# Expansion units of the next head pair between the first score steps of this one

## The chip, the cores and the metric

The kernel runs on one core of a Trainium2 chip. The time is device microseconds (us) of one execution of the program. Three executions of the kernel before took 3314.32, 3317.00 and 3317.49 us; the median is 3317.0 us. The profile is of a further execution, which took 3313.17 us; its span, from the first to the last instruction, is 3311.3 us. The engines are TensorE (PE; PEld is its weight load), VectorE (DVE), ScalarE (ACT), GpSimd (POOL) and the queue SyncE (SP).

## The reference, cut to what matters

Two layers over 1024 latent and 128 context tokens of width 1024: a short gated convolution and a multi-head latent attention, each followed by a squared-ReLU MLP. The change touches only the attention of the second layer. It has 16 heads of 96 query and key values (64 plus 32 rotary) and 64 values:

```python
q = (rmsnorm(h @ w_dq, q_norm_g) @ w_uq).reshape(b, n, N_HEADS, QK_DIM);  q = rmsnorm(q, qn_g)
kn, v = jnp.split((ckv @ w_ukv).reshape(b, n, N_HEADS, QK_NOPE + V_DIM), [QK_NOPE], axis=-1)
k = rmsnorm(jnp.concatenate([kn, kpe], -1), kn_g)          # then the rotary part of q and k
s = jnp.einsum('bqhd,bkhd->bhqk', qblk, k) * scale
p = jax.nn.softmax(s, axis=-1);  o = jnp.einsum('bhqk,bkhd->bqhd', p, v)
```

The latent tokens attend to themselves and to 128 cached keys, the context tokens to themselves.

## The kernel before, in words

Every product of 32-bit values is made of three matmuls (`three`, L814 to L822): each operand is kept as a high part and a low part, and high*high, high*low and low*high are summed. ACT makes the high parts, DVE or GpSimd the low ones.

The heads are worked in 8 pairs. Seven pairs run in a hardware loop, the eighth is written out with `last=True`. Each engine has its own program of a pair, and semaphores tie them. The parts of a pair are:

- **Value units.** 3 units of TensorE (60 matmuls of 128x128) make v of both heads for all 10 key tiles; ACT and DVE take it out as v_hi and v_lo.
- **Turn units of head 1.** 6 units of transposes turn q_tok (9 tiles) and k_tok (10 tiles) into qT and kT; ACT makes qT_hi and kT_hi, DVE qT_lo and kT_lo.
- **Expansion units** (`qk_units`, 8 units). They make q and k of the *next* pair: 5 query units (81 matmuls of 192 columns) and 3 key units (60 of 128 columns). ACT copies each to q_tok or k_tok and squares it in place in PSUM, DVE sums the squares (ssq). On DVE the program puts between the sums the normalisation of the previous pair (`over_sums`, 5 pieces: a reciprocal of the row sums, and a multiplication of o), and the rotary part of the queries (`rotate`, twice).
- **Score steps.** Positions 0 to 37, 19 of each head: 18 of 512 columns and one of 128. Position pos makes scores of position pos+3 (3 matmuls into bank 3 or 4), and the values product of position pos (3 matmuls). Between them stand ACT's exponential p and its high part p_hi (`step`), and GpSimd's low part p_lo.
- **Maxima.** 9 tiles of each head: 3 matmuls write 1152 columns into banks 0 to 2 (`max_tile`), DVE reduces them to row_max (`max_out`). There is one buffer, so a tile waits for the reduction of the one before. Then row_max is transposed (`max_unit`) and DVE writes it as extra rows of qT_hi (`max_rows`); the scores of that head read these rows. Head 1's maxima are for this pair, head 0's for the next.
- **Token scaling** (`token_scale`). DVE divides q_tok and k_tok by their norms (r_tok), in parts between the reductions of head 1. ACT's square root for r_tok (`token_rstd`) needs another table than the exponential.
- **Turn units of head 0** of the next pair, at TURN_A.

All units share banks 0 to 2 in turn (`unit`): unit k waits until unit k-3 has been taken out. The maxima use the same banks, so the first tile of a head waits until every unit is taken out. The order of the work is written out by hand, per engine, by positions: before, the 8 expansion units all come ahead of position 0, a maxima tile comes every one and a half positions from position 0 and from 22 on, row maxima follow at 13 and 35, the turn of head 0 at 20. The first scores of the next pair are made at positions 36 and 37. ACT writes out sums and products of head 0 (`output`) after its steps 17, 21 and 22.

## Time and profile before

| what | value |
|---|---|
| median of three runs | 3317.0 us |
| profiled execution, and its span | 3313.17 us, 3311.3 us |
| TensorE busy | 3070.7 us, 93% of the span |
| VectorE, ScalarE, GpSimd busy | 1469.5, 1011.1, 855.9 us |
| slices of the span with TensorE at 7 to 8 tenths | those of the attention (about 1500 to 2370 us) |

A busy time is an average over stages with different limits. In the slices of the two MLPs TensorE shows 9 tenths or more; in those of the attention 7 or 8. "Idle before" in a row is the time in which the engine did nothing before the instruction, and the name behind the arrow is what ended that wait. Matmuls overlap, so the duration of a single one is longer than its share; the start of one to the start of the next is the share.

### The profile page before, as it was taken

How to read it: one execution, taken by the hardware profiler on the slowest of the kernel's cores; microseconds unless marked ns; L12 is line 12 of the kernel's file. 1: busy time of each engine (PE TensorE's matmuls, PEld its weight loads, DVE VectorE, ACT ScalarE, POOL GpSimd, SP SyncE). 2: the span in 40 equal slices, each digit the busy share in tenths (PEclk: the TensorE clock that was granted, in tenths of full speed). 3: DMA queues.
4: the chain of work that ended last, by engine and by line, in shares of the span. 5: the costliest groups of instructions: out<-in, count | busy, mean ns of one | idle time of the engine just before them, and what ended most of it. 6: DMA issues, size and time to landing. Idle time of an engine off the chain costs nothing.

```text
span 3311.3 us, 43718 instructions
## 1 busy us (share of the span) xinstructions
PE 3070.7 (93%) x17193; PEld 2931.1 (89%) x17193; DVE 1469.5 (44%) x1856; ACT 1011.1 (31%) x1447; POOL 855.9 (26%) x509
## 2 busy tenths in 40 slices
PE   7999998999999999877888888888898999999999
PEld 7999998999999999876777777776798999999999
DVE  2654545555544556554455554564324222222222
ACT  2211113111111112223666667556613111111111
POOL 0122111212212121111553446445421112212121
PEclk6999998999999999886999999899999999999999
DMA  4122220222111221200000000000110111111111
GB/s 192 66 84 94 75 90 32 77 77 82 63 69 64 89 76 63 93 11 7 6 7 2 7 5 7 8 6 0 77 44 26 45 39 44 44 38 39 44 44 76
DMA packets 45532, 166.60 MB, mean 50 GB/s; under 512 B 5792, under 2 KB 7456, under 8 KB 45216
## 3 DMA queue, kind: packets, MB, share of 16 engines
q1 hardware_dynamic: 44912, 160.89, 13.9%
q10 hardware_dynamic: 560, 4.87, 0.4%
q8 instruction: 43, 0.70, 0.1%
q14 instruction: 17, 0.14, 0.0%
HBM read 156.15 MB, written 9.58 MB: 50 GB/s over the span
## 4 chain that ended last, share of the span: by engine, by line
PE 61%; issue 23%; DVE 9%; ACT 4%; POOL 2%; DVEq 0%; ACTq 0%; POOLq 0%
PE ps L822 58%; PE ps L1068 2%; POOL w_lo L459 2%; DVE sums L1586 2%; DVE row_max L1568 1%; ACT p L745 1%; DVE hid_lo L1306 1%; DVE tmp L1301 1%; PE ps L1054 1%; ACT hid_hi L594 1%; ACT tmp L591 1%; DVE q_tok L1543 1%; DVE ssq L1508 0%; DVE k_tok L1548 0%; DVE x L1272 0%
## 5 line engine op out<-in xcount | busy, mean ns | idle before, releaser
L459 POOL TENSOR_TENSOR w_lo<-w_raw,w_hi 128x1024 fp32r<-128x1024 f32 (+2 forms) x190 | 463.4, 2439 | 1979.0 <-ACT w_hi L532 1979.0
L822 PE MATMUL ps<-h_hi,w_hi 128*128 128x384 f32 x2640 | 607.7, 338 | 49.5 <-DVE h_lo L1253 24.6
L822 PE MATMUL ps<-h_lo,w_hi 128*128 128x384 f32 x2640 | 604.2, 336 | 0.0
L822 PE MATMUL ps<-h_hi,w_lo 128*128 128x384 f32 x2640 | 603.1, 336 | 0.0
L822 PEld LDWEIGHTS ps<-h_hi,w_hi 128*128 128x128 f32 x2640 | 474.6, 190 | 54.0 <-issue 43.7
L475 POOL TENSOR_TENSOR p_lo<-p,p_hi 128x512 fp32r<-128x512 f32 (+1 forms) x304 | 384.2, 1273 | 433.8 <-ACT p_hi L747 429.8
L532 ACT ACTIVATE w_hi<-w_raw 128x1024 fp32r<-128x1024 f32 (+2 forms) x190 | 194.6, 1025 | 984.1 <-PE ps L822 912.1
L822 PEld LDWEIGHTS ps<-h_lo,w_hi 128*128 128x128 f32 x2640 | 475.4, 190 | 0.0
L822 PEld LDWEIGHTS ps<-h_hi,w_lo 128*128 128x128 f32 x2640 | 474.2, 189 | 0.0
L1272 DVE SCALAR_TENSOR_TENSOR x<-ps,mod,x 128x256 f32<-128x256 f32 (+5 forms) x432 | 240.1, 611 | 480.0 <-PE ps L822 478.3
L822 PE MATMUL ps<-hid_hi,w_hi 128*128 128x384 f32 x1536 | 350.4, 335 | 9.7 <-DVE hid_lo L1306 9.6
L822 PE MATMUL ps<-hid_lo,w_hi 128*128 128x384 f32 x1536 | 348.6, 334 | 0.0
L822 PE MATMUL ps<-hid_hi,w_lo 128*128 128x384 f32 x1536 | 348.5, 334 | 0.0
L1301 DVE SCALAR_TENSOR_TENSOR tmp<-ps,tmp 128x1152 f32<-128x1152 f32 x64 | 86.9, 1358 | 494.3 <-ACT tmp L591 494.3
L822 PEld LDWEIGHTS ps<-hid_hi,w_hi 128*128 128x128 f32 x1536 | 272.6, 188 | 15.1 <-DVE hid_lo L1306 14.7
L822 PEld LDWEIGHTS ps<-hid_lo,w_hi 128*128 128x128 f32 x1536 | 273.7, 188 | 0.0
L822 PEld LDWEIGHTS ps<-hid_hi,w_lo 128*128 128x128 f32 x1536 | 273.7, 188 | 0.0
L1568 DVE TENSOR_REDUCE row_max<-ps 128x1 f32<-128x1152 f32 x144 | 178.1, 1237 | 159.0 <-PE ps L1068 159.0
L591 ACT ACTIVATE tmp<-ps 128x1152 f32<-128x1152 f32 x64 | 72.6, 1135 | 531.6 <-PE ps L822 531.6
L745 ACT ACTIVATE p<-ps 128x512 f32<-128x512 f32 (+1 forms) x304 | 175.8, 578 | 160.1 <-PE ps L822 152.2
L1189 DVE CUSTOM_DVE_ANT_0 ps<-mod_raw,cond_row 128x1024 f32<-128x1024 f32 x80 | 211.7, 2646 | 1.6 <-issue 0.7
L747 ACT ACTIVATE p_hi<-p 128x512 fp32r<-128x512 f32 (+1 forms) x304 | 187.0, 615 | 9.7
(135 smaller groups left out, 3587.3 us busy)
## 6 DMA issues: line engine op xcount, KB each, us to landing
w_raw<-in_wall_dram SPq DMA_DIRECT2D x174, 512.0 KB, 3.7
mod_raw<-in_mod_rows_dram SPq DMA_DIRECT2D x80, 512.0 KB, 3.5
mod_first<-in_mod_cols_dram SPq DMA_DIRECT2D x16, 512.0 KB, 15.2
x<-in_x_t_dram SPq DMA_DIRECT2D x8, 576.0 KB, 7.6
x_spill<-x ACTq DMA_DIRECT2D x1, 4608.0 KB, 15.2
x<-x_spill SPq DMA_DIRECT2D x1, 4608.0 KB, 13.7
out_dram<-x SPq DMA_DIRECT2D x8, 576.0 KB, 2.8
w_raw<-in_wall_dram SPq DMA_DIRECT2D x8, 416.0 KB, 3.1
```

Source lines behind the costliest of these rows:

```text
L459: pool.tensor_tensor(w_lo[s][:, 0:words], w_raw[s][:, 0:words], w_hi[s][:, 0:words].bitcast(F32), ALU.subtract).then_inc(w_lo_done, 1)
L475: pool.tensor_tensor(p_lo[s][:, 0:n], p32[s][:, 0:n], p_hi[s][:, 0:n].bitcast(F32), ALU.subtract).then_inc(p_lo_done, 1)
L532: act.activation(w_hi[s][:, 0:words], w_raw[s][:, 0:words], ACT.Copy).then_inc(w_hi_done, 1)
L591: act.activation(cols3(tmp[0][:, 0:N]), stage_ps(L.at["s"]), ACT.Relu).then_inc(relu_done, 1)
L745: act.activation(p32[s][:, 0:n], bank(3 + pos % 2, n), ACT.Exp, scale=SCALE).then_inc(p_exp, 1)
L747: act.activation(p_hi[s][:, 0:n], p32[s][:, 0:n], ACT.Copy).then_inc(p_hi_done, 1)
L822: ins = pe.matmul(out, lhs[a], rhs[b](cols), start=first and n == 0, stop=last and n == 2)
L1068: ins = pe.matmul(ps[:, b0:b0 + n], qT_hi[s][0:QK, t * P:(t + 1) * P], kT_hi[s][0:QK, c0:c0 + n], start=True, stop=True)
L1189: ins = dve.tensor_tensor_reduce(product, raw, cond_row[:, c, :], 1.0, 0.0, ALU.mult, ALU.add, mod_acc[:, slot, c:c + 1])
L1272: ins = dve.scalar_tensor_tensor(xt, v, mod[:, ds(gate, 1), c:c + 1].rearrange("p a c -> p (a c)"), xt, ALU.mult, ALU.add)
L1301: dve.scalar_tensor_tensor(cols3(tmp[1][:, 0:N]), stage_ps(L.at["s"]), 0.0, cols3(tmp[0][:, 0:N]), ALU.max, ALU.mult).then_inc(stage_free, 1)
L1568: dve.tensor_reduce(row_max[:, t:t + 1], ps[:, 0:n], AX_X, ALU.max).then_inc(max_free, 1)
```

## The change: what it does

The table EXPAND says after which position which expansion unit stands: units 0 and 1 after position 0, units 2 to 7 after positions 1 to 6. A maxima tile comes every position instead of every one and a half; head 1's start at position 7 instead of 0, head 0's at 23 instead of 22. Row maxima follow at 15 and 32 instead of 13 and 35. The turn of head 0 is at 21 instead of 20. The first two scores of the next pair come after position 37. On ACT the square root comes after step 11 instead of 4, and the outputs of head 0 after steps 14, 26 and 27. On DVE the scaling parts become 7 instead of 5 (each key part is split in two) and stand behind tiles 2 to 8. The names `expand`, `q_unit`, `k_unit`, `kv_unit`, `turn_queries` and `turn_keys` cut the old loops into single units; what a unit does is the same.

```diff
-TURN_A = STEPS + 1
-MAX_B, MAX_A = 0, TURN_A + 2
-ROWS_B, ROWS_A = MAX_B + 13, MAX_A + 13
+EXPAND = [(0, 0), (0, 1), (1, 2), (2, 3), (3, 4), (4, 5), (5, 6), (6, 7)]
+TURN_A = STEPS + 2
+MAX_B, MAX_A = 7, TURN_A + 2
+ROWS_B, ROWS_A = MAX_B + 8, MAX_A + 9
...
@@ ACT, pair()
                             turn_units(U_V, 1)
-                            if not last:
-                                qk_units(U_V + U_TURN)
-                        if pos == LAG + 1 and not last:
+                        for at_pos, i in EXPAND:
+                            if pos == at_pos + LAG and not last:
+                                expand(U_V + U_TURN, i)
+                        if pos == LAG + 8 and not last:
                             token_rstd()
...
-                        if pos in (17, STEPS + 9 + LAG):
+                        if pos in (14, STEPS + 9 + LAG):
                             output(head, 0, p)
-                        if pos in (17 + LAG + 1, 18 + LAG + 1):
-                            output(0, pos - 17 - LAG, p)
+                        if pos in (TURN_A + 5, TURN_A + 6):
+                            output(0, pos - TURN_A - 4, p)
...
@@ PE, pair()
                     turn_units(U_V, 1)
                     if not last:
-                        qk_units(U_V + U_TURN)
                         A.at["tok"] += 1
-                    pe.wait_ge(unit_free, A.count("u", (0 if last else U_QK) + U_TURN))
+                    pe.wait_ge(unit_free, A.count("u", U_TURN))
                     def maxima(half):
 
                         for s, start in ((1, MAX_B), (0, MAX_A)):
-                            t, off = divmod(half - 2 * start, 3)
+                            t, off = divmod(half - 2 * start, 2)
...
                         if pos + LAG < 2 * STEPS:
                             scores(pos + LAG)
-                        elif pos > 2 * STEPS - LAG and not last:
-                            scores(pos - (2 * STEPS - LAG + 1), LAG - 1)
                         maxima(2 * pos)
                         values(pos)
                         maxima(2 * pos + 1)
+                        for at_pos, i in EXPAND:
+                            if pos == at_pos and not last:
+                                expand(U_V + U_TURN, i)
...
+                    if not last:
+                        for pos in range(LAG - 1):
+                            scores(pos, pos)
...
@@ DVE, token_scale() and pair()
-                    elif part == 3:
-                        scale_keys(0)
+                    elif part in (3, 5):
+                        scale_keys((part - 3) // 2)
                     else:
-                        scale_keys(1).then_inc(tok_ready, 1)
+                        ins = rotary_keys((part - 4) // 2)
+                        if part == 6:
+                            ins.then_inc(tok_ready, 1)
...
-                        if not last and 2 <= t < 7:
+                        if not last and t >= 2:
                             token_scale(t - 2)
```

VectorE, the end of head 1's maxima in the loop. Each TENSOR_REDUCE of row_max is one tile; the TENSOR_TENSOR rows are the scaling of q_tok and k_tok; the last row but one before is the writing of the row maxima. Before, from tile 5 on:

```order
L1568 TENSOR_REDUCE row_max<-ps 128x1
L1548 TENSOR_TENSOR k_tok<-k_tok,r_tok 128x10x64
L1549 TENSOR_TENSOR k_tok<-kpe_rot,r_tok 128x10x32
L1567 REGISTER_ALU
L1568 TENSOR_REDUCE row_max<-ps 128x1
L1548 TENSOR_TENSOR k_tok<-k_tok,r_tok 128x10x64
L1549 TENSOR_TENSOR k_tok<-kpe_rot,r_tok 128x10x32
L1567 REGISTER_ALU
L1568 TENSOR_REDUCE row_max<-ps 128x1
L1567 REGISTER_ALU
L1568 TENSOR_REDUCE row_max<-ps 128x1
L1573 REGISTER_ALU
```

After, from tile 6 on, to the writing of the row maxima:

```order
L1638 TENSOR_REDUCE row_max<-ps 128x1
L1617 TENSOR_TENSOR k_tok<-kpe_rot,r_tok 128x10x32
L1637 REGISTER_ALU
L1638 TENSOR_REDUCE row_max<-ps 128x1
L1613 TENSOR_TENSOR k_tok<-k_tok,r_tok 128x10x64
L1637 REGISTER_ALU
L1638 TENSOR_REDUCE row_max<-ps 128x1
L1617 TENSOR_TENSOR k_tok<-kpe_rot,r_tok 128x10x32
L1643 REGISTER_ALU
L1645 SCALAR_TENSOR_TENSOR qT_hi_106<-ps,ident 9x1152
```

The key parts have moved behind the last tiles: a scaling operation now stands between the last reduction and the writing of the row maxima.

TensorE, the end of head 1's maxima. `ident,row_max` is the transposition of the row maxima, `qT_hi_106` and `kT_hi_110` belong to head 1, whose first scores (position 19) they make. Before, what stands around the transposition:

```order
L822 MATMUL ps<-qT_hi_105,kT_hi_109 128x512
L822 MATMUL ps<-qT_lo_107,kT_hi_109 128x512
L822 MATMUL ps<-qT_hi_105,kT_lo_111 128x512
L822 MATMUL ps<-p_hi_118,v_hi 128x512
L822 MATMUL ps<-p_lo_117,v_hi 128x512
L822 MATMUL ps<-p_hi_118,v_lo 128x512
L1075 REGISTER_ALU
L1007 REGISTER_ALU
L1077 MATMUL ps<-ident,row_max 9x128
```

After:

```order
L1114 MATMUL ps<-kT_hi_110,qT_hi_106 128x128
L841 MATMUL ps<-p_hi_115,v_hi 128x512
L841 MATMUL ps<-p_lo_114,v_hi 128x512
L841 MATMUL ps<-p_hi_115,v_lo 128x512
L1121 REGISTER_ALU
L1026 REGISTER_ALU
L1123 MATMUL ps<-ident,row_max 9x128
L1131 REGISTER_ALU
L1133 REGISTER_ALU
L841 MATMUL ps<-qT_hi_106,kT_hi_110 128x512
L841 MATMUL ps<-qT_lo_108,kT_hi_110 128x512
```

Before, positions 14 and 15 stood between the transposition and head 1's first scores; now those scores follow it at once.

ScalarE, ahead of the turn of head 0 (`qT_hi`); `o` and `sums` are an output. Before:

```order
L760 ACTIVATE o_87<-ps 64x512
L761 ACTIVATE sums<-ps 64x512
L743 REGISTER_ALU
L745 ACTIVATE p_1_116<-ps 128x512
L747 ACTIVATE p_hi_118<-p_1_116 128x512
L759 REGISTER_ALU
L760 ISA
L760 ACTIVATE o_87<-ps 64x128
L761 ACTIVATE sums<-ps 64x128
```

After:

```order
L763 ACTIVATE p_2_119<-ps 128x512
L765 ACTIVATE p_hi_121<-p_2_119 128x512
L528 REGISTER_ALU
L533 ACTIVATE w_hi_76<-w_raw_74 128x1024
L761 REGISTER_ALU
L763 ACTIVATE p_0_113<-ps 128x512
L765 ACTIVATE p_hi_115<-p_0_113 128x512
L690 REGISTER_ALU
L691 ACTIVATE qT_hi_105<-ps 96x512
```

The two outputs have gone behind the turn, and the splitting of a weight block (w_hi), which stood behind the turn, has come one step ahead of it.

## Rows read from the trace of the kernel before

**Rows 1.** The page, busy time, share of the span and instructions
```profile
PE 3070.7 (93%) x17193; PEld 2931.1 (89%) x17193; DVE 1469.5 (44%) x1856; ACT 1011.1 (31%) x1447; POOL 855.9 (26%) x509
```

**Rows 2.** Busy time by stretch: pairs 2 to 7 together; pair 4 alone
```profile
1628.05:2276.05 648.00, 565.85 (x3115) 473.87 (x3115) 347.59 (x414) 417.13 (x750) 307.34 (x240) 0.96 0.02 5
1845.98:1951.98 106.00, 92.06 (x520) 76.89 (x520) 57.91 (x69) 69.45 (x125) 51.25 (x40) 0.98 0.02 5
```

**Rows 3.** Timeline of TensorE in pair 4: start, length, in brackets idle before
```profile
1858.62 1.46 PE L1054 MATMUL ps<-ident,k_tok 128*96 128x128 f32 x10 [1.57 <-DVE qT_lo L1478]
1860.81 0.36 PE L822 MATMUL ps<-w_hi,ql_hi 128*128 128x192 f32 x1 [0.74 <-DVE kT_lo L1498]
...
1881.14 0.79 PE L1068 MATMUL ps<-kT_hi,qT_hi 96*128 96x512 f32 x3 [3.43 <-DVE ssq L1508]
...
1890.88 0.50 PE L822 MATMUL ps<-qT_hi,kT_hi 105*128 105x512 f32 x1 [1.36 <-ACT p L745]
...
1904.42 0.80 PE L1068 MATMUL ps<-kT_hi,qT_hi 96*128 96x512 f32 x3 [1.20 <-DVE row_max L1568]
...
1908.04 0.33 PE L1068 MATMUL ps<-kT_hi,qT_hi 96*128 96x128 f32 x1 [0.69 <-DVE row_max L1568]
...
1924.31 1.46 PE L1054 MATMUL ps<-ident,k_tok 128*96 128x128 f32 x10 [3.06 <-DVE qT_lo L1478]
...
1951.98 0.49 PE L822 MATMUL ps<-qT_hi,kT_hi 105*128 105x512 f32 x1 [1.52 <-DVE qT_hi L1575]
```

**Rows 4.** Busy time by stretch: the expansion units of pair 4
```profile
1860.81:1876.80 15.99, 15.99 (x142) 15.89 (x142) 13.06 (x18) 6.35 (x15) 0.00 (x0) 1.00 0.00 0
```

**Rows 5.** Chain of waits in pair 4: a maxima tile, one and a half steps
```profile
1927.85 0.52 PE ps L1068 x3
1928.36 2.12 PE ps L822 x9
```

**Rows 6.** Timeline of TensorE ahead of the loop, at half clock
```profile
1491.08 1.33 PE L1068 MATMUL ps<-kT_hi,qT_hi 96*128 96x512 f32 x3 [1.45 <-DVE row_max L1568]
```

**Rows 7.** Timeline of VectorE in pair 4, reductions and scalings
```profile
1894.37 1.92 DVE L1543 TENSOR_TENSOR q_tok<-q_tok,r_tok 128x864 f32<-128x864 f32 x1
1896.21 1.34 DVE L1568 TENSOR_REDUCE row_max<-ps 128x1 f32<-128x1152 f32 x1
1897.48 1.04 DVE L1543 TENSOR_TENSOR q_tok<-q_tok,r_tok 128x864 f32<-128x864 f32 x1
...
1899.71 1.90 DVE L1548 TENSOR_TENSOR k_tok<-k_tok,r_tok 128x640 f32<-128x640 f32 x1
1901.53 1.57 DVE L1549 TENSOR_TENSOR k_tok<-kpe_rot,r_tok 128x320 f32<-128x320 f32 x1
...
1904.29 0.92 DVE L1548 TENSOR_TENSOR k_tok<-k_tok,r_tok 128x640 f32<-128x640 f32 x1
1905.13 1.58 DVE L1549 TENSOR_TENSOR k_tok<-kpe_rot,r_tok 128x320 f32<-128x320 f32 x1
```

**Rows 8.** Timeline of GpSimd in pair 4
```profile
1901.29 1.46 POOL L475 TENSOR_TENSOR p_lo<-p,p_hi 128x512 fp32r<-128x512 f32 x1 [0.36 <-ACT p_hi L747]
```

**Rows 9.** Timeline of VectorE ahead of the loop, GpSimd idle
```profile
1478.31 2.03 DVE L1543 TENSOR_TENSOR q_tok<-q_tok,r_tok 128x864 f32<-128x864 f32 x2
...
1480.99 0.49 DVE L1549 TENSOR_TENSOR k_tok<-kpe_rot,r_tok 128x320 f32<-128x320 f32 x1
...
1482.13 0.48 DVE L1549 TENSOR_TENSOR k_tok<-kpe_rot,r_tok 128x320 f32<-128x320 f32 x1
```

**Rows 10.** Timeline of ScalarE in pair 4
```profile
1886.99 1.28 ACT L735 ACT_TABLE_LOAD   x1
...
1926.53 1.05 ACT L532 ACTIVATE w_hi<-w_raw 128x1024 fp32r<-128x1024 f32 x1
1927.48 0.59 ACT L745 ACTIVATE p<-ps 128x512 f32<-128x512 f32 x1
1928.10 0.63 ACT L747 ACTIVATE p_hi<-p 128x512 fp32r<-128x512 f32 x1
```

**Rows 11.** Timeline of TensorE in the last pair
```profile
2291.93 0.79 PE L1068 MATMUL ps<-kT_hi,qT_hi 96*128 96x512 f32 x3 [1.10 <-DVE kT_lo L1498]
...
2303.22 1.33 PE L1068 MATMUL ps<-kT_hi,qT_hi 96*128 96x512 f32 x3 [8.35 <-DVE row_max L1568]
```

More of the change, by code:

```diff
@@ L1047, in turn_units, with q_unit @@
[L1047 to L1057 removed]
+                def q_unit(k, i):
+                    if i == 0:
+                        weights()
+                    a, z = groups(NT, 2)[i]
+                    b0 = unit(k)
+                    for t in range(a, z):
+                        out = ps[:, b0 + (t - a) * 2 * QK:b0 + (t - a + 1) * 2 * QK]
+                        for kt in range(QT):
+                            cols = slice(kt * 2 * QK, (kt + 1) * 2 * QK)
+                            ins = three([(out, 0)], kt, kt == 0, kt == QT - 1,
+                                        [r[:, kt, t * P:(t + 1) * P] for r in (ql_hi, ql_lo)],
+                                        [lambda _, w=w: w[:, cols] for w in (w_hi[0], w_lo[0])])
+                    unit_end(ins)
@@ new lines, in qk_units, with kv_unit @@
+                def qk_units(k):
+                    for i in range(5):
+                        q_unit(k + i, i)
+                    kv_units(k + 5, 0, QT * 2 * QK)
+                def kv_unit(k, slot, w0, i):
+                    a, z = groups(KTILES, 4)[i]
+                    b0 = unit(k)
+                    for t in range(a, z):
+                        out = ps[:, b0 + (t - a) * 2 * VD:b0 + (t - a + 1) * 2 * VD].rearrange(
+                            "p (h n) -> p h n", h=2)
+                        for kt in range(CT):
+                            ins = three([(out, 0)], kt, kt == 0, kt == CT - 1,
+                                        [r[:, kt, t * P:(t + 1) * P] for r in (ckv_hi, ckv_lo)],
+                                        [lambda _, w=w: w[:, w0:w0 + 2 * CT * VD].rearrange(
+                                            "p (h k n) -> p h k n", h=2, k=CT)[:, :, kt, :]
+                                         for w in (w_hi[slot], w_lo[slot])])
+                    unit_end(ins)
+                    if i == 2:
+                        L.at["b"] += 1
@@ new lines, in kv_units, with turn_unit @@
+                def kv_units(k, slot, w0):
+                    for i in range(3):
+                        kv_unit(k + i, slot, w0, i)
+                def turn_unit(k, head, src, tiles):
+                    a, z = tiles
+                    b0 = unit(k)
+                    for t in range(a, z):
+                        ins = pe.transpose(ps[0:QK, b0 + (t - a) * P:b0 + (t - a + 1) * P],
+                                           src[:, t, head, :], ident[:, :])
+                    unit_end(ins)
@@ new lines, in turn_queries, with turn_keys @@
+                def turn_queries(k, head):
+                    pe.wait_ge(tok_ready, A.count("tok"))
+                    for i in range(3):
+                        turn_unit(k + i, head, q_tok, groups(NT, 4)[i])
+                def turn_keys(k, head, i):
+                    turn_unit(k, head, k_tok, groups(KTILES, 4)[i])
+                def turn_units(k, head):
+                    turn_queries(k, head)
+                    for i in range(3):
+                        turn_keys(k + 3 + i, head, i)
@@ L1059, in max_tile, with expand @@
+                def expand(k, i):
+                    if i < 5:
+                        q_unit(k + i, i)
+                    else:
+                        kv_unit(k + i, 0, QT * 2 * QK, i - 5)
                 def max_tile(s, t):
@@ L1525, in qk_units, with expand @@
                                       ALU.add).then_inc(ssq_done, 1)
+                def qk_units(k):
+                    for i in range(5):
+                        q_unit(k + i, i)
+                    k_units(k + 5)
+                def expand(k, before):
+                    for i in range(5):
+                        q_unit(k + i, i)
+                        if before is not None:
+                            over_sums(i, before)
+                    k_units(k + 5)
                 def rotate(h):
@@ L1598, in pair @@
                     if not last:
-                        qk_units(U_V + U_TURN, before if not first else None)
+                        expand(U_V + U_TURN, before if not first else None)
                     else:
@@ L1616, in _ @@
                 qk_units(0)
-                for part in range(5):
+                for part in range(7):
                     token_scale(part)
```

135 lines of the change are left out of this document (57 added, 78 removed).

## The prediction, made before the changed kernel was run

> **What bounds the kernel now.** I read the page first: TensorE is busy 93% of the span [rows 1], and only the slices of the attention show it at 7 or 8 tenths, so a change there is worth what TensorE idles or runs slowly there. Then the busy time by stretches: pairs 2 to 7 take 648.00 us, 108.0 each, at a mean granted clock of 0.96; pair 4 takes 106.00 at 0.98 [rows 2]. The clock has two levels, 1.2 and 2.4 GHz, so 0.98 means that 2% of the pair, 2.1 us, is lost to the lower one. A mean pair loses that and the 2.0 us by which it is longer, 4.1 us in all. Third, the timeline of TensorE in pair 4 with its idle times: 1.57, 0.74, 3.43, 1.36, 1.20, 0.69, 3.06 and 1.52 us [rows 3], 13.6 us of 106. The reader is to see the names behind the arrows: nearly all end on DVE. The rest of the pair is matmuls that the change only moves, so it can win these 13.6 us and the clock, and nothing else.
>
> The largest wait, 3.43, stands behind the expansion units. They occupy TensorE for 15.99 us without a break [rows 4], in which DVE is busy 13.06 us and still has sums, normalisation and rotary work queued when TensorE asks for the first maxima tile. GpSimd does nothing in that stretch (0.00), since no score step runs: that is a reserve, and below it is also a danger.
>
> **The change part by part**, for one of pairs 2 to 7.
>
> *Removed, 12.0 us.* 0.74 goes: the units now stand behind a score step and a values step, which last 2.12 x 6/9 = 1.41 us together [rows 5], while DVE finishes kT_lo. 3.43 goes: seven steps of 1.41 and 16.0 us of units give 25.9 us of TensorE work, and DVE's share, the 13.06 and what follows it until the tile at 1881.14 (4.3 us at most), fits in. 1.36 goes: it is ACT's square root with two table loads of 1.28 [rows 10], at a time when ACT had only just got its first scores. Now it comes after step 11, where three steps with a tile each (1.41 + 0.52, 1.93 [rows 5]) pass until TensorE needs exponential 12; ACT needs 1.22 for its step, 2 x 1.28 for the tables, the short root itself and 0.59, under 5 us in all. 1.20 and 0.69 go with the old order of the tiles. 3.06 goes with the outputs that stood in ACT's queue ahead of qT_hi. 1.52 goes: the row maxima of head 0 are ready five positions before they are read. That is 0.74 + 3.43 + 1.36 + 1.20 + 0.69 + 3.06 + 1.52 = 12.0. The first 1.57 stays; nothing around it changes.
>
> *Added (a), first tile of head 1.* It waits until key unit 7 is taken out, and TensorE puts only one score product of 0.7 us between them; against it stand two operations of ACT and one of DVE on a half-size unit, an estimated 1.1 (no row here is of exactly that pair). That is 0.4; below it is bounded by 0. If the rotary work of the unit before is late by one GpSimd operation of 1.46 [rows 8], it is 1.9. I take 0.9.
>
> *Added (b), tiles of head 1 at one per step.* From the end of a tile on TensorE to the start of the next, the reduction takes 1.45 us [rows 6]; with the tile itself, 1.33/2 at full clock, that is a cycle of 2.12 against TensorE's own 1.93. That holds for three cycles, 6.4 us; reduction 3 starts at 7.1. From there DVE is the bound: a reduction takes 1.27 from its start to the start of the next operation [rows 7], so tiles 3 to 7 give 5 x 1.27 = 6.35, tile 8 of 128 columns 0.27, the six scalings S, and the writing of the row maxima 1.35. TensorE waits for the last one, because head 1's first scores are the next thing in its queue: 7.1 + 6.35 + 0.27 + 1.35 + 0.05 = 15.1 + S. Its own work in the same time is 8 x 1.93, plus 1.0 for the last tile, product and transposition, minus 0.4 for the short step: 16.0. Queued behind this wait is the whole of head 1, so every us counts.
>
> S has two measured ends. In the loop the six last 1.92 + 1.04 + 1.90 + 1.57 + 0.92 + 1.58 = 8.93 [rows 7], less 0.08 of overlap each, 8.45. Ahead of the loop, with GpSimd idle, they last from 1478.31 to 1482.61, 4.30 [rows 9]. The same rotary part takes 1.57 and 0.49. The row of 1901.53 ends at 1903.10, 0.35 after GpSimd's operation of 1901.29 ends (1902.75) [rows 7, 8]: DVE with two inputs in SBUF waits for GpSimd's operation to end, and then takes its 0.4. So each scaling costs its own time plus what is left of a p_lo. An upper bound is a whole 1.29 us for each of the six: 12.0. I take S = 6.5: with DVE as the bound a step lasts 2.1 to 3.1 us instead of 1.9, so a p_lo is under way about half of the time, and a scaling started right after a reduction often comes before it. That is between the two rows. It makes the wait 15.1 + 6.5 - 16.0 = 5.6; with 8.45 it is 7.5, with 4.3 it is 3.4, with 12.0 it is 11.1.
>
> The Trainium skill has this as a rule: "GPSIMD Engine Reference", section 1 Specifications, says that the SBUF interfaces are shared with VectorE, with contention for VectorE instructions in a 2-port mode or with two SBUF inputs. By that rule the row above agrees, and the rule speaks against the change, which brings the rotary and normalising work beside p_lo. The price I take from rows: the rotary work of units 5 and 6 has slack in (a), the scalings in (b) have none.
>
> *Added (c), turn of head 0.* 1.57 as at the first turn, plus the weight block's split (1.05) that now stands one step ahead, less ACT's slack of a step, 1.41 - 1.22 (0.59 and 0.63 [rows 10]): 2.4.
>
> *Added (d), tiles of head 0.* Eight cycles, 2.12 - 1.93 each: 1.5. Between zero and twice that.
>
> *The clock.* A mean pair loses 4.1 us to the lower level. It fell after waits such as the 3.43 and the 3.06. The longest waits left are the one at the end of (b), some 2.7 us, and 2.4, shorter but of the same kind. I count half of the loss, 2.0, as won; the ends are 0 and 4.1.
>
> *Sum of a pair:* 12.0 - 0.9 - 5.6 - 2.4 - 1.5 = 1.6, plus 2.0, is 3.6 us. Six pairs: 21.6. The first pair normalises no earlier one, so its DVE queue is short already: I count 0.
>
> *Last pair.* There the waits are 1.10 and 8.35 [rows 11], because five pieces of normalisation (about 10 us) stand on DVE ahead of the reductions while the tiles began at position 0. Now seven steps, 9.9 us, run first. The tile behind the 8.35 took 1.33 at half clock, so some 2 us of slow matmuls go too. New are 0.6, 7 x 0.19 and 1.5 for the row maxima ahead of position 19. 11.4 - 3.4 = 8.0.
>
> *Total:* 21.6 + 8.0 = 29.6. The profiled execution of 3313.2 would become 3283.6. It was 3.8 below the median of the runs, so the time is 3287.
>
> **The rivals.**
> 1. *The idle time only changes its name.* The scalings keep their price in the loop (S = 8.45) and the clock loses as much as now. A pair then wins 1.6 - 1.9 = -0.3, the six nothing, the last pair 8: 3317 - 8 + 2 = 3311. For it speaks that the scaling rows repeat in every pair; against it that they follow a pile of p_lo behind the table loads.
> 2. *DVE and GpSimd fall out of step and the clock stays up.* S = 4.3 and all of the 4.1 is won: a pair wins 1.6 + 2.2 + 4.1 = 7.9, six 47, the last 8: 3262. For it speaks that no wait of over 3 us is left; against it that several waits now stand close together.
> 3. *Slower.* Every scaling waits for a whole p_lo, since TensorE lets a score step go just as DVE starts one: S = 12.0, a pair loses 5.5 - 1.6 = 3.9 and wins no clock. Six pairs: +23.4, less 8: 3332. With the clock unchanged it decides against the change from S = 6.5 + 1.6 + 1.3 = 9.4 on, not far above the 8.45 measured. Against it: two of six scalings in the loop ran at their own time.
> 4. *The change doesn't reach the timeline* (a unit still waits for all the others, by its bank): 3317. The order of the engines speaks against it.
>
> **How the numbers follow.** Chances: forecast 0.47, rival 1 0.17, rival 2 0.24, rival 3 0.09, rival 4 0.03. The forecast's own range, by (a), (c), (d) and the clock, is 3272 to 3300. For 8 in 10 I go down past rival 2 halfway (3257) and up over rival 1 (3316). A measurement of this kernel can tell about 0.2%, 6.6 us, from no change. Faster takes the forecast, rival 2 and about half of rival 1: 0.80. Same takes the other half and rival 4: 0.11. Slower: 0.09.
>
> **What would show it.** In the profile after: in a pair of the loop no wait for ssq above 1.5 us; the wait for r_tok's table loads gone from TensorE's rows; a wait of 2 to 3 us before position 19 that ends on DVE's qT_hi, with waits for row_max of 0.3 to 1.2 ahead of it; 2.4 instead of 3.06 at the turn; none before position 0's scores; pairs 2 to 7 of 104.4 on the mean; in the last pair no wait of 8 us. The forecast is wrong if pairs stay above 107 (rivals 1 and 3: look at the lengths of the scaling rows), if they are below 102 (rival 2: the granted clock at 0.99 or more), or if a new wait stands in positions 0 to 6, where I expect none: then the rotary work beside GpSimd or the three banks of the units are the cause.

## The result, and the profile after

The changed kernel takes 3295.65 us, the median of four runs (3293.13 to 3297.1), against 3315.66 for the kernel before in the same session (3310.38 to 3317.49): a ratio of 0.9941, with a 95% interval of 0.9924 to 0.9959. That is 20.0 us less; 29.6 were forecast, 3287 with a range of 3257 to 3316. The span of the profiled execution fell by 16.0 us, from 3311.3 to 3295.3. The two profiled executions are not the medians (3313.17 us before, 3297.1 after), so the rows below have 16 of the 20 us to explain.

The page of the kernel after, busy time, answers to [rows 1]:

```profile
PE 3087.7 (94%) x17193; PEld 2916.4 (89%) x17193; DVE 1470.8 (45%) x1856; ACT 1012.0 (31%) x1447; POOL 859.2 (26%) x509
```

Busy time by stretch of the kernel after: pairs 2 to 7 together, pair 4 alone, and the 6.9 us behind position 19's first scores. The columns are those of [rows 2]: TensorE, its weight load, VectorE, ScalarE, GpSimd, then the granted clock.

```profile
1627.48:2262.27 634.79, 578.71 (x3115) 461.13 (x3115) 347.85 (x414) 417.66 (x750) 309.62 (x241) 0.97 0.02 5
1839.00:1944.84 105.84, 96.50 (x520) 76.93 (x520) 57.97 (x69) 69.61 (x125) 51.55 (x41) 0.97 0.02 5
1902.71:1909.60 6.89, 6.88 (x20) 5.55 (x21) 0.00 (x0) 2.50 (x5) 1.27 (x1) 0.58 0.00 0
```

A pair of the six takes 105.8 us, where 108.0 were needed before and 104.4 forecast. The third row is new: in each of the six pairs the clock falls to its lower level there.

The mean of 108.0 hides an uneven loop. Five pairs of the kernel before, from the first expansion product of one to that of the next, take 111.1, 106.8, 106.0, 106.2 and 111.0 us. These are the first and the third, busy time by stretch:

```profile
1642.88:1754.01 111.13, 97.82 (x519) 82.41 (x519) 58.06 (x70) 69.66 (x126) 51.18 (x40) 0.92 0.02 5
1860.81:1966.81 106.00, 92.05 (x520) 76.90 (x520) 57.91 (x70) 69.46 (x126) 51.25 (x40) 0.98 0.02 5
```

The granted clock is 0.92 in one and 0.98 in the other, 17.1 and 3.4 us at the lower level. After the change all five take 105.8 us. So 10.5 of the 12.1 us that the five pairs win come from the two slow ones, and pair 4, whose rows the prediction priced, wins 0.2.

Timeline of TensorE in pair 4 of the kernel after, only rows with idle time of 0.25 us or more; it answers to [rows 3]:

```profile
1851.63 1.46 PE L1080 MATMUL ps<-ident,k_tok 128*96 128x128 f32 x10 [1.57 <-DVE qT_lo L1527]
1879.87 0.80 PE L1114 MATMUL ps<-kT_hi,qT_hi 96*128 96x512 f32 x3 [0.53 <-DVE ssq L1563]
1888.61 0.50 PE L841 MATMUL ps<-qT_hi,kT_hi 105*128 105x512 f32 x1 [0.50 <-ACT p L763]
1894.37 0.79 PE L1114 MATMUL ps<-kT_hi,qT_hi 96*128 96x512 f32 x3 [0.58 <-DVE row_max L1638]
1898.86 0.33 PE L1114 MATMUL ps<-kT_hi,qT_hi 96*128 96x128 f32 x1 [0.42 <-DVE row_max L1638]
1902.71 0.79 PE L841 MATMUL ps<-qT_hi,kT_hi 105*128 105x512 f32 x1 [2.58 <-DVE qT_hi L1645]
1916.89 1.46 PE L1080 MATMUL ps<-ident,k_tok 128*96 128x128 f32 x10 [2.34 <-DVE qT_lo L1527]
1943.37 0.50 PE L841 MATMUL ps<-p_hi,v_hi 128*128 128x512 f32 x1 [0.27 <-POOL p_lo L476]
1944.84 0.50 PE L841 MATMUL ps<-p_hi,v_hi 128*128 128x512 f32 x1 [0.50 <-POOL p_lo L476]
```

The reader is to see that 0.74, 3.43 and 1.52 of before are gone, that 1.36 has become 0.50 and the 1.20 and 0.69 between the tiles 0.58 and 0.42, and that 2.58 before position 19 and, in place of 3.06, 2.34 at the turn of head 0 stand there nearly as forecast (2.7 and 2.4). The last two rows were not forecast: the scores of the next pair no longer stand between the last values products of this one, and those of positions 35 and 36 wait for p_lo.

Timeline of VectorE, the end of head 1's maxima in the same pair: the last rotary part, and the writing of the row maxima:

```profile
1896.47 0.48 DVE L1617 TENSOR_TENSOR k_tok<-kpe_rot,r_tok 128x320 f32<-128x320 f32 x1
...
1899.65 1.55 DVE L1617 TENSOR_TENSOR k_tok<-kpe_rot,r_tok 128x320 f32<-128x320 f32 x1
1901.23 1.35 DVE L1645 SCALAR_TENSOR_TENSOR qT_hi<-ps,ident 9x1152 fp32r<-9x1152 f32 x1
```

The same operation has 0.48 and 1.55, as in [rows 7, 9]. The six scalings take 1.05, 1.63, 0.81, 0.48, 0.81 and 1.55, 6.33 in all, S = 5.85 after 0.08 of overlap each (6.5 forecast).

In the last pair TensorE waits 1.57 us at the turn, as before. Its longest waits besides are these, for 1.10 and 8.35 before [rows 11]:

```profile
2292.16 1.33 PE L1114 MATMUL ps<-kT_hi,qT_hi 96*128 96x512 f32 x3 [3.46 <-DVE row_max L1638]
2312.34 0.50 PE L841 MATMUL ps<-qT_hi,kT_hi 105*128 105x512 f32 x1 [1.44 <-DVE qT_hi L1645]
```

### The profile page after: what moved, and what is told of

Same layout as the page of the kernel before. It is cut to its first block, busy times and chain, and to the rows that moved or that the text cites. A ratio compares the mean times of both kernels' runs of the same rounds, so it can differ in the third digit from the quotient of the medians.

```text
span 3295.3 us, 43718 instructions
## 1 busy us (share of the span) xinstructions
PE 3087.7 (94%) x17193; PEld 2916.4 (89%) x17193; DVE 1470.8 (45%) x1856; ACT 1012.0 (31%) x1447; POOL 859.2 (26%) x509
## 3 DMA queue, kind: packets, MB, share of 16 engines
q1 hardware_dynamic: 44912, 160.89, 13.9%
## 4 chain that ended last, share of the span: by engine, by line
PE 48%; issue 33%; POOL 12%; DVE 4%; ACT 2%; POOLq 0%; DVEq 0%; ACTq 0%
PE ps L841 47%; POOL p_lo L476 10%; POOL w_lo L460 2%; DVE hid_lo L1355 1%; DVE tmp L1350 1%; ACT hid_hi L595 1%; ACT tmp L592 1%; DVE x L1321 0%; DVE ps L1238 0%; PE ps L937 0%; ACT tmp L540 0%; DVE sums L1656 0%; POOLq L475 0%; PE ps L1114 0%; PE ps L931 0%
## 6 DMA issues: line engine op xcount, KB each, us to landing
x<-x_spill SPq DMA_DIRECT2D x1, 4608.0 KB, 13.7
```

## The experiments

Twelve kernels were run. All but one start from the changed kernel (3295.65). Unless an edit says otherwise, the rest is as in the diff above. "Before" was 3316.24 us in the session of the first four, 3314.61 for the next four, 3316.26 for the three after and 3315.03 for the last. The changed kernel wasn't measured again in the later sessions; the kernel before moved by 1.6 us between them.

The table compares them by what the loop shows. Period, idle time and half clock are means of five pairs, from the first expansion product of pair 2 to that of pair 7. Idle is the sum of the bracketed times of TensorE's timeline. Half clock is the time at the lower level, worked out as twice what the granted clock lacks to 1, times the length. These columns are of the profiled execution, the times are medians: that of the extra matmuls was 5.1 us above its median, the others lie within 2.7 us of theirs except that of the cut turns (5.0 below, with runs 33 us apart).

| kernel | time | ratio to before, 95% | period | idle | half clock |
|---|---|---|---|---|---|
| before | 3315.66 | | 108.2 | 13.7 | 9.6 |
| changed | 3295.65 | 0.9924 to 0.9959 | 105.8 | 9.3 | 6.8 |
| outputs alone, on before | 3294.53 | 0.9926 to 0.9951 | 105.8 | 11.7 | 8.9 |
| outputs back | 3316.06 | 0.9995 to 1.0012 | 108.5 | 10.3 | 9.6 |
| units ahead of position 0 | 3317.49 | 0.9995 to 1.0013 | 109.2 | 9.5 | 13.7 |
| units in a block behind 0 | 3296.51 | 0.9928 to 0.9953 | 105.8 | 8.8 | 6.8 |
| scores back | 3294.64 | 0.9926 to 0.9953 | 105.6 | 8.8 | 6.8 |
| last scaling behind rows | 3289.16 | 0.9909 to 0.9936 | 104.6 | 8.2 | 5.5 |
| extra matmuls | 3282.09 | 0.9885 to 0.9915 | 103.9 | 7.0 | 1.4 |
| slower tiles of head 0 | 3279.87 | 0.9877 to 0.9907 | 103.5 | 9.3 | 5.5 |
| zeros for p_lo | 3271.08 | 0.9852 to 0.9881 | 102.6 | 7.4 | 3.4 |
| three together | 3260.52 | 0.9828 to 0.9853 | 100.9 | 7.1 | 2.1 |
| cut turns | 3282.50 | 0.9877 to 0.9930 | 102.9 | 5.9 | 7.5 |
| cut turns, earlier | 3238.43 | 0.9759 to 0.9786 | 97.5 | 3.9 | 0.0 |

**The wait before position 19: one scaling part behind the row maxima.**

```diff
-                        if not last and t >= 2:
+                        if not last and 2 <= t < 8:
                             token_scale(t - 2)
                     max_rows(U_V + U_TURN + U_QK, 1)
                     if not last:
+                        token_scale(6)
```

> The changed kernel with one edit: the last scaling part of k_tok (1.55 us beside GpSimd) stands on VectorE behind the writing of head 1's row maxima instead of ahead of it. Theory A (the fall of TensorE's clock in every pair comes from the idle time of 2.58 us ahead of head 1's first scores): the wait shrinks to about 1.4 us, the clock stays at its upper level in the pairs, and a pair takes 105.8 - 1.2 - 3.2 = 101.4 us, the kernel about 3295 - 7 x 4.4 = 3264. Rival B (the clock falls for what the whole stretch of maxima does, or at any wait over 1 us): the half-clock stretch of 6.8 us stays in each pair, a pair takes 104.6, the kernel about 3287.

Measured: 3289.16, 6.5 us less: rival B's 3287, not theory A's 3264. TensorE, before position 19 and at the turn behind it:

```profile
1898.41 0.77 PE L841 MATMUL ps<-qT_hi,kT_hi 105*128 105x512 f32 x1 [1.52 <-DVE qT_hi L1645]
1911.55 2.11 PE L1080 MATMUL ps<-ident,k_tok 128*96 128x128 f32 x10 [2.34 <-DVE qT_lo L1527]
```

The wait falls by 1.06, yet half clock stays at 5.5 us a pair: the ten transpositions take 2.11 instead of 1.46, so the lower level now also stands at the turn. The scaling part was on the path, and the clock came back by a fifth only.

**Extra matmuls in that wait.** Ten products without use, placed between the row maxima's transposition and head 1's first scores.

```diff
                             max_unit(U_V + U_TURN + U_QK)
+                            if not last:
+                                for n in range(FILL):
+                                    pe.matmul(ps[:, n % 2 * BANK:(n % 2 + 1) * BANK], qT_hi[1][0:QK, 0:P],
+                                              kT_hi[1][0:QK, 0:BANK], start=True, stop=True)
```

> The changed kernel with ten matmuls of 512 columns more per pair, right behind the transposition of head 1's row maxima; they write banks 0 and 1, which nobody reads then, and last about 2.2 us, less than the wait of 2.58 that follows. They add no wait and take none away; outputs are unchanged. Theory A (the clock falls because TensorE is idle there): the clock stays up, a pair takes 105.8 - 3.3 = 102.5 us, the kernel about 3295 - 7 x 3.3 = 3272. Rival B (the fall has another cause): the half-clock stretch stays, the pair stays at 105.8 or grows, since the added matmuls run at whatever clock there is: 3295 to 3300.

Measured: 3282.09, 13.6 us less, with more work on the same path.

```profile
1897.90 2.55 PE L1185 MATMUL ps<-kT_hi,qT_hi 96*128 96x512 f32 x10
1900.74 0.49 PE L842 MATMUL ps<-qT_hi,kT_hi 105*128 105x512 f32 x1 [0.29 <-DVE qT_hi L1650]
```

The scores start 3.87 us after head 1's last tile, as in the changed kernel (3.85); only the idle time became work, and half clock fell from 6.8 to 1.4 us a pair. 5.4 us at half clock are 2.7 us of lost work; the period fell by 1.9. So the lower level is a cost of its own, which follows TensorE's idle stretch and not VectorE's lateness. Theory A put it at 23 us, which is too much: in two of the five pairs 3.4 us of half clock now stand at the turn of head 0. In the other three the clock stays at its full level, although TensorE waits 2.33 us there.

**The tiles of head 0, one to one and a half steps again.**

```diff
-                        for s, start in ((1, MAX_B), (0, MAX_A)):
-                            t, off = divmod(half - 2 * start, 2)
+                        for s, start, every in ((1, MAX_B, 2), (0, MAX_A, 3)):
+                            t, off = divmod(half - 2 * start, every)
```

> The changed kernel, but head 0's maxima tiles come every one and a half positions again (from position 23; row maxima after position 35), head 1's stay at one a position. Theory A (at one a position every tile waits: cycle 2.24 against TensorE's 1.93): the eight waits of 0.31 go, a pair takes 105.8 - 2.5 = 103.3 us, the kernel about 3278. Rival B (with the waits gone TensorE runs into ScalarE or GpSimd, whose p_lo of 1.29 and the outputs stand in the same positions): the time comes back as waits for p_lo at the end of the pair, which grow from 0.77 to 2 us or more, and the kernel gains less than 8 us.

Measured: 3279.87, 15.8 us less, 2.3 us a pair. At one per step a cycle of tiles took 2.24 us, 15.69 for the seven from 1922.42 to 1938.11, against 1.93 of TensorE's own; this is a wait that no bracket shows. Some of the 2.3 us is the clock: half clock fell by 1.4 us, 0.7 of work. The three pairs that still have 6.8 us of it take 104.0 us, so the tiles alone are worth 1.8. At one and a half the cycle is hidden, at the price of two waits that end the pair:

```profile
1933.28 0.33 PE L1114 MATMUL ps<-kT_hi,qT_hi 96*128 96x128 f32 x1 [0.35 <-DVE row_max L1638]
1935.91 0.50 PE L841 MATMUL ps<-qT_hi,kT_hi 105*128 105x512 f32 x1 [0.46 <-DVE qT_hi L1645]
```

**The first scores of the next pair back at positions 36 and 37.**

```diff
                             scores(pos + LAG)
+                        elif pos > 2 * STEPS - LAG and not last:
+                            scores(pos - (2 * STEPS - LAG + 1), LAG - 1)
...
-                    if not last:
-                        for pos in range(LAG - 1):
-                            scores(pos, pos)
```

> The changed kernel, but the first two scores of the next pair stand at positions 36 and 37 again, ahead of the values products. Theory A: the two waits of the values products for p_lo at the end of a pair (0.27 and 0.50 us) go, a pair takes 105.0, the kernel about 3290. Rival B: ScalarE's outputs of the pair's end come 1.4 us later with the values products, and the value units of the next pair wait for ScalarE; no change or slower, 3295 to 3300.

Measured: 3294.64, the same within the intervals. Of the two new waits at the pair's end the one of 0.50 goes and the one of 0.27 stays (0.26). That edit is worth nothing measurable.

**Zeros instead of the low part of p.**

```diff
-                pool.tensor_tensor(p_lo[s][:, 0:n], p32[s][:, 0:n], p_hi[s][:, 0:n].bitcast(F32),
-                                   ALU.subtract).then_inc(p_lo_done, 1)
+                pool.tensor_tensor(p_lo[s][:, 0:32], p32[s][:, 0:32], p_hi[s][:, 0:32].bitcast(F32), ALU.subtract)
+                pool.memset(p_lo[s][:, 32:n].bitcast(F32), 0.0).then_inc(p_lo_done, 1)
```

> GpSimd subtracts only 32 columns of each p and writes zeros to the other 480, so the low part of p is left out of 15/16 of the attention; TensorE's, VectorE's and ScalarE's instructions are as in the changed kernel. Theory A: VectorE's scalings of two SBUF inputs are long (S = 5.85 us a pair, a key's rotary part 1.63 and 1.55) because each waits for the end of a GpSimd operation of two SBUF inputs. Then each rotary part falls to about 0.5, S to about 4.3, the wait of 2.58 before position 19 to about 1.0, and the two waits for p_lo at the pair's end (0.27 and 0.50) go; with half of the clock's 2.6 us a pair wins some 3.5, the last pair some 2: about 3273. Rival B: the scalings are long for a reason of their own (the operands' layout, the wait for the reduction before): their lengths stay, the 2.58 stays, and only the 0.8 at the pair's end is won: about 3291.

Measured: 3271.08, 24.6 us less. VectorE's last rotary part, GpSimd's two operations, and TensorE before position 19:

```profile
1891.03 0.54 DVE L1617 TENSOR_TENSOR k_tok<-kpe_rot,r_tok 128x320 f32<-128x320 f32 x1
```

```profile
1890.96 0.25 POOL L476 TENSOR_TENSOR p_lo<-p,p_hi 128x32 fp32r<-128x32 f32 x1 [1.55 <-ACT p_hi L765]
1891.16 0.50 POOL L477 MEMSET p_lo<- 128x480 f32 x1
```

```profile
1893.08 0.49 PE L841 MATMUL ps<-qT_hi,kT_hi 105*128 105x512 f32 x1 [1.56 <-DVE qT_hi L1645]
```

The rotary part falls from 1.55 in the changed kernel to 0.54 although GpSimd's memset runs beside it; it starts at 1891.03, while the 32 columns are being subtracted. So the price of a scaling is what is left of GpSimd's reading operation. Theory A holds for that. The wait fell to 1.56 and not to 1.0, and of the 6.8 us at half clock 3.4 went. Not all of the 24.6 us is the scalings': GpSimd's own time for a p_lo fell too, from 1.28 to 0.70.

The Trainium skill, "SBUF — State Buffer", section "Who interferes with whom", says that a VectorE instruction with two SBUF inputs contends with a GpSimd instruction that reads SBUF, and not with one that only writes it. These rows agree: 1.55 beside p_lo's subtraction, 0.54 beside the memset.

**The expansion units ahead of position 0 again**, all else as changed.

```diff
-EXPAND = [(0, 0), (0, 1), (1, 2), (2, 3), (3, 4), (4, 5), (5, 6), (6, 7)]
+EXPAND = []
@@ ACT and PE, pair()
                     turn_units(U_V, 1)
+                    if not last:
+                        qk_units(U_V + U_TURN)
```

> The eight expansion units stand again without a break ahead of position 0, all else as changed (maxima from position 7, one to a step). Theory A (as in the forecast): what won was that seven score steps now lie between the units and the first maxima tile, in whatever order; with the units ahead, the 3.43 us wait for the sums stays away, the 0.74 us wait ahead of the units returns, and the 0.53 before the first maxima tile goes. Then a pair costs some 0.2 to 0.5 us more: 3296 to 3299. Rival B: the interleaving itself carries the gain, by leaving TensorE no stretch in which it outruns VectorE and ScalarE: then ScalarE and GpSimd idle through the 16 us of units, the waits behind them come back, and the time goes back towards 3310.

Measured: 3317.49, the whole gain is gone. But the waits are those of theory A: 0.74 is back, the wait for ssq is away, and idle time is 9.5 us a pair, as in the changed kernel (9.3). The period is 3.4 us longer. Busy time by stretch, from the units' first matmul on:

```profile
1861.17:1868.00 6.83, 6.83 (x32) 6.83 (x33) 2.73 (x4) 0.99 (x3) 0.00 (x0) 0.50 0.00 0
```

Behind the waits of 1.57 and 0.74 there are 6.8 more us of half clock, in every pair: 3.4 us of work, which is the difference. Neither theory named this.

**The units in one block behind position 0.**

```diff
-EXPAND = [(0, 0), (0, 1), (1, 2), (2, 3), (3, 4), (4, 5), (5, 6), (6, 7)]
+EXPAND = [(0, i) for i in range(8)]
```

> All eight expansion units stand without a break behind position 0 (in the run with the units ahead of position 0 the whole gain was gone: 3317.5, with a stretch of half clock of 6.8 us behind the waits of 1.57 and 0.74 us in every pair). Theory A: it was that second wait that cost, 0.74 us and the clock behind the pair of waits; a score step and a values step between the turn and the units take it away, the stretch of half clock goes too, and the time is that of the changed kernel, 3294 to 3299. Rival B: the unbroken block costs, since the work of ScalarE, VectorE and GpSimd piles up behind it; then the waits and the time come out like those with the block ahead of position 0: 3310 to 3318.

Measured: 3296.51, the changed kernel's time, with the same 6.8 us of half clock. Strewing the units between seven steps is worth nothing; one step between the turn and the units is worth the 21 us between these two runs.

**The outputs of head 0 back in front of the turn.**

```diff
-                        if pos in (14, STEPS + 9 + LAG):
+                        if pos in (17, STEPS + 9 + LAG):
                             output(head, 0, p)
-                        if pos in (TURN_A + 5, TURN_A + 6):
-                            output(0, pos - TURN_A - 4, p)
+                        if pos in (17 + LAG + 1, 18 + LAG + 1):
+                            output(0, pos - 17 - LAG, p)
```

> The outputs of head 0 stand again after steps 17, 21 and 22 on ScalarE, ahead of the turn of head 0, all else as changed. Each is two operations of 0.57 and 0.59 us. Theory A: they push ScalarE back by up to 1.1 us at the turn (its slack of a step is 0.19 us), so that the wait of 2.34 us there becomes 3.0 to 3.4, as it was before the change (3.06): 0.7 to 1.0 us a pair, 3300 to 3302. Rival B: ScalarE catches up while TensorE makes the transposes, the wait stays at 2.34 and the time at 3296.

Measured: 3316.06, the whole gain is gone here too. TensorE at the turn, and the stretch from there on:

```profile
1928.65 2.37 PE L1080 MATMUL ps<-ident,k_tok 128*96 128x128 f32 x10 [3.05 <-DVE qT_lo L1527]
```

```profile
1928.65:1934.40 5.75, 5.75 (x19) 4.88 (x20) 2.62 (x5) 2.42 (x5) 1.53 (x2) 0.50 0.25 74
```

The wait is 3.05, as theory A said, 0.7 us more. The time is 20.4 us more, four times what that wait explains over seven pairs: a stretch of half clock stands behind it. By the table a pair has 1.0 us more of idle time and some 2.7 more of half clock (1.4 of work), together 2.4 of the 2.7 by which the period grew.

**The outputs alone, on the kernel before.**

```diff
-                        if pos in (17, STEPS + 9 + LAG):
+                        if pos in (14, STEPS + 9 + LAG):
                             output(head, 0, p)
-                        if pos in (17 + LAG + 1, 18 + LAG + 1):
-                            output(0, pos - 17 - LAG, p)
+                        if pos in (TURN_A + 5, TURN_A + 6):
+                            output(0, pos - TURN_A - 4, p)
```

> The kernel before with one part of the change alone: on ScalarE the outputs of head 0 stand after steps 14, 25 and 26 instead of 17, 21 and 22. Theory A: the outputs ahead of the turn cost 0.7 us of waiting at the turn (3.06 becomes 2.3 to 2.4) and, in the pairs that have it, the stretch of half clock behind that wait, so a pair wins 0.7 to 2.5 us, the seven 5 to 17: 3300 to 3311. Rival B: here the turn stands at 20, not 21, and what makes 3.06 is the units' banks and the score step ahead; the wait keeps its length and the time stays at 3313 to 3318.

Measured: 3294.53, as fast as the whole change, and below the range of either theory.

```profile
1872.81 0.78 PE L1068 MATMUL ps<-kT_hi,qT_hi 96*128 96x512 f32 x3 [2.91 <-DVE ssq L1508]
...
1913.88 1.46 PE L1054 MATMUL ps<-ident,k_tok 128*96 128x128 f32 x10 [1.63 <-DVE qT_lo L1478]
```

The turn waits 1.63 instead of 3.06 [rows 3], 1.4 us less (0.7 expected). Idle time falls by 2.0 us a pair in all and half clock from 9.6 to 8.9, 0.4 us of work, together the 2.4 us by which the period fell. The gain is not even here either: these five pairs take 104.8 to 106.5 us, so pair 4's 106.0 is not bettered, and what goes are the pairs of 111. In those two the clock had fallen at the turn, about 1 us before its wait of 3.07 ended (pair 4 has the same wait at full clock); with 1.63 it falls at the turn in no pair. The expansion units, the tiles and the scaling parts add nothing to these moved lines.

**Three together**: the scaling part behind the rows, the slower tiles of head 0, and five extra matmuls (FILL = 5).

> Three edits of the earlier runs together: the last scaling part behind the row maxima's writing (alone 3289.2), head 0's tiles one to one and a half steps (alone 3279.9), and half as many extra matmuls before position 19, five (ten alone: 3282.1). Theory A: their gains are of different kinds and add up, 6.5 + 15.8 + 13.5 = 36 us less what the first and third share in the same wait, about 6: 3266. Rival B: most of each gain is the same one, the lower clock level behind the wait before position 19, which can be won only once: about 3278.

Measured: 3260.52. Alone they won 6.5, 15.8 and 13.6 (with ten), 35.9 in sum; together 35.1. They add up; theory A had expected the first and third to share about 6 us of the same wait.

**The turns cut in two.** On top of the three: keys' transposes behind the next steps, both turns; MAX_A = TURN_A + 3; the second weight block's split six steps later.

```diff
-                    turn_units(U_V, 1)
+                    turn_queries(U_V, 1)
...
+                        if pos == 0:
+                            for i in range(3):
+                                turn_keys(U_V + 3 + i, 1, i)
...
-                                turn_units(k, 0)
+                                turn_queries(k, 0)
+                            if pos == TURN_A + 1:
+                                for i in range(3):
+                                    turn_keys(k + 3 + i, 0, i)
```

> On top of the three edits together (3260.5): both turns are cut in two, the queries' transposes as now, the keys' behind the next score step and values step; the tiles of head 0 start one position later, and the split of the second weight block stands six steps later. Theory A: the waits at the turns (1.57 and 2.33 us) are the latency from transposes through ScalarE and VectorE, and work of TensorE's own between them (1.41 us) hides most of it: 1.57 becomes 0.2 to 0.5, 2.33 becomes about 1, and the stretches of half clock at the turn go: 3 to 4 us a pair, 3235 to 3242. Rival B: what is late at the turn is ScalarE's queue, which the cut doesn't shorten; the wait then moves behind the next step at its old length, and only the clock may change: 3255 to 3262.

Measured: 3282.50, above both theories and 22 us more than without the cut, with runs from 3266.95 to 3300.3. TensorE's waits at the end of the maxima of head 0, and then two stretches: the one behind these waits, and a later pair from its units to those of the next:

```profile
1839.51 0.33 PE L1124 MATMUL ps<-kT_hi,qT_hi 96*128 96x128 f32 x1 [0.70 <-DVE row_max L1658]
1842.12 0.50 PE L851 MATMUL ps<-qT_hi,kT_hi 105*128 105x512 f32 x1 [1.04 <-DVE qT_hi L1665]
```

```profile
1842.20:1860.00 17.80, 17.80 (x79) 16.86 (x79) 1.81 (x3) 6.76 (x12) 2.50 (x2) 0.52 0.00 0
1963.72:2062.94 99.22, 93.44 (x525) 76.19 (x525) 56.99 (x70) 69.31 (x126) 51.33 (x40) 1.00 0.02 6
```

Idle time fell, from 7.1 to 5.9 us a pair, by less than theory A asked: the waits at the turns are gone, but 1.1 to 1.7 us for kT_lo ahead of the units are new. Three of the loop's six pairs (two of the five in the table) have 17.1 to 20.5 us of half clock in one stretch, the others none, with the same waits of 0.7 and 1.1 ahead. What decides between them stays open. A pair without takes 99.2.

**The same, one position earlier**: TURN_A = STEPS + 1, and expansion units 0 to 3 after positions 1 and 2.

> The version with the cut turns (3282.5), with the turn of head 0 and its tiles one position earlier (20 and from 23, so that the row maxima are ready at 35, two positions before the next pair's first scores), and expansion units 0 to 3 after positions 1 and 2 instead of 0 and 1, so that the 1.1 us wait for kT_lo ahead of them has a step more. Theory A: in three of the five pairs measured the clock fell for some 10 to 20 us behind the waits of 0.71 and 1.1 us at the row maxima of head 0; the other pairs took 99.2 us. Without those two waits every pair takes about 99: against the 100.9 of the three edits 1.9 us less in each of seven pairs: 3243 to 3250. Rival B: what let the clock fall is the row of short waits as such, which the cut turns spread over the pair; then it still falls in some pairs and the time is not below 3260, with runs that differ by 10 us or more.

Measured: 3238.43 (3235.6 to 3239.35), 57.2 us below the changed kernel and 76.6 below the one before. Pair 4, and TensorE at the turn of head 0 and at the end of head 0's maxima:

```profile
1829.80:1927.30 97.50, 93.47 (x526) 76.11 (x526) 55.67 (x70) 69.44 (x126) 51.63 (x40) 1.00 0.02 6
```

```profile
1885.27 1.46 PE L1090 MATMUL ps<-ident,k_tok 128*96 128x128 f32 x10 [0.25 <-DVE qT_lo L1547]
...
1910.36 0.33 PE L1124 MATMUL ps<-kT_hi,qT_hi 96*128 96x128 f32 x1 [0.36 <-DVE row_max L1658]
1913.00 0.50 PE L851 MATMUL ps<-qT_hi,kT_hi 105*128 105x512 f32 x1 [0.46 <-DVE qT_hi L1665]
```

The period is 97.5 us. No wait longer than 0.61 us is left in a pair, and the clock is at its full level in all of them. More than the two waits was changed, so it isn't shown that they alone had let the clock fall. It still holds the five extra matmuls of each pair; whether it needs them wasn't tried.

## Why the prediction was right, and what in it was wrong

- **Removed, 12.0: nearly right.** Six of the seven waits went, with the new ones that (a) to (d) told in their places; of the 1.36 behind the table loads 0.50 stayed.
- **(a) 0.9:** 0.53. **(c) 2.4:** 2.34.
- **(b) 5.6:** from the first tile (1879.87) to position 19's scores (1902.71) are 22.84 us, against 16.0 of TensorE's own: 6.8. S was well placed (5.85 for 6.5), and the zeros for p_lo showed its mechanism. With that S the sum would have been 5.0, so the stretch was 1.9 us longer elsewhere: the first three cycles took 2.24 instead of 2.12, the 0.50 is in it, and VectorE itself stood waiting for tiles, 0.42 and 0.49 us, where the forecast had it busy without a break.
- **(d) 1.5 was too small:** a cycle takes 2.24, not 2.12, so nine tiles cost about 2.4. The run with the slower tiles gives 1.8 us a pair for them at equal clock, after paying 0.8 of waits at the pair's end.
- **Missed:** 0.77 us of waiting for p_lo at the pair's end, where I had expected none before position 0's scores. I had not priced that positions 35 and 36 lose the scores between their values products.
- **The last pair, 8.0, gave 3.7.** From its first value product to its last values product of 512 columns it took 77.4 us instead of 81.1. The five pieces of normalisation now run beside seven p_lo, and a multiplication takes 1.06 instead of 0.43, so 3.46 us of the 8.35 are left. It is the same contention that I had priced in (b); here I had counted VectorE's queue by its lengths without GpSimd.
- **The clock, 2.0:** half clock fell from 9.6 to 6.8 us a pair, 1.4 us of work (of 4.8, where I had counted 4.1). As a size that is near. As a mechanism it is the term that decides, and I had treated it as a remainder: the pairs of the kernel before differ by 5 us at nearly the same idle time (13.3 to 13.9), and the gain lies in the two that had 17.1 us of half clock. The new stretch of 6.8 us at the wait that (b) makes has no term in the sum.

With the measured sizes a pair wins 12.0 - 0.5 - 6.3 - 2.3 - 2.4 - 0.8 - 0.5 + 1.4 = 0.6 (the 0.5 of the table loads is taken out of (b)); the periods say 2.2 to 2.4. Some 1.7 us of the gain are not placed. An estimate the other way round, from the table: without half of the half clock a pair took 103.4 us before and 102.4 after, so the waits give 1.0 (1.6 forecast) and the clock 1.4 (2.0 forecast).

So the time lay in the range, 9 us above the forecast, and in part by luck: the terms that were too small and those that are not placed partly cancel. The ledger behind it was not a cause. I had grouped the outputs with the turn, 3.06 against 2.4, and given the gain to the whole rearrangement. The runs show the moved outputs as sufficient (3294.5 alone) and as necessary (3316.1 without them). The rest of the change takes away some 8 us of waits in a pair and makes as many: 3294.5 and 3295.6. And two edits that each bring back about 1 us of waiting or less lose all 20 us, because each brings back a stretch of half clock. Rival 1 (the idle time only changes its name) tells what all the parts but the outputs came to, though not by its reason: it had S at 8.45, and S was 5.85.

## What to carry to other kernels

Where TensorE idles in several places, write beside each wait what clock it has behind it, and forecast the two together: here a wait of 0.7 us was worth 20. Before a rearrangement is credited, run its smallest part alone; here the smallest part did it all. Look at every pair, not at the mean: half or more of a gain can lie in a few iterations that happened to run at the lower clock. And shorter waits in sum don't promise a better clock: with the cut turns idle time fell, and the clock fell for 17 to 20 us in half of the pairs. Only the kernel whose waits were all under 0.7 us stayed at full clock in every pair.

## What the runs showed of the hardware that was not expected

- The granted clock fell at the wait of 2.58 us in every pair of the changed kernel, and behind 1.57 and 0.74 us with 1.46 us of transposes between them in every pair from 2 on with the units ahead of position 0, but not behind 1.57 us alone in the changed kernel. The length of a wait alone doesn't tell: in pair 4 of the kernel before the 3.06 us at the turn stand at full clock (1921.25 to 1935.00 at 1.00). In the kernel before, 1.57 and 0.74 stood in the same place and the clock fell there in some pairs only, not in pair 4 [rows 4].
- A stretch of half clock in the loop lasted 3.4 or 6.8 us in most variants, and 17.1 or 20.5 us in pairs of the kernel with the cut turns. There half clock makes TensorE's own work longer and nothing waits, so nothing in the brackets shows it.
- Ten matmuls a pair whose result nobody reads, put into a wait of 2.58 us, made the kernel 13.6 us faster.
- The same VectorE operation of two SBUF inputs takes 0.54 us beside a GpSimd memset and 1.55 beside a subtraction.
